# Expert mixture of a hybrid block: accumulator kept turned, 288-token additions, and the further items' round on weights that are still in the ring

## What is computed

```python
# x (1, 512, 1024) float32, 16 meta tokens ahead, D_MODEL 1024, 64 experts, TOP_K 6, D_EXPERT 256
h = layer_norm(concat([meta, x]))
m = hybrid_mixer(h)                      # one projection, HGRN2, RG-LRU, output projection
h = layer_norm(ALPHA * h + m)
scores = sigmoid(h @ router_w)
idx = top_k(scores + router_bias, 6)
wts = scores[idx] / sum(scores[idx]) * 2.5
h = layer_norm(ALPHA * h + swiglu(h, shared) + sum over e in idx of wts_e * swiglu(h, expert e))
# swiglu(x) = (silu(x @ w_gate) * (x @ w_up)) @ w_down
return h[:, 16:]
```

## Time and profile before

| | us |
|---|---|
| median of 3 runs | 1144.53 (1142.01 to 1144.99) |
| the profiled execution: its own time | 1144.19 |
| its span, first to last instruction | 1142.2 |
| first gate and up of an expert pair starts | 589.57 |
| finish starts | 1120.87 |
| PE busy | 1109.3 (97% of the span) |
| DVE busy | 723.1 (63%) |
| moved by DMA | 286.70 MB |

### The profile page before, as it was taken

How to read it: one execution, slowest core, us unless ns; L and a number is a source line. 1 busy time by engine, 2 the same in 40 slices (tenths; PEclk the granted TensorE clock), 3 DMA queues, 4 the chain that set the end, 5 groups by cost and what they waited for, 6 DMA issues and landing times.

```text
span 1142.2 us, 19416 instructions
## 1 busy us (share of the span) xinstructions
PE 1109.3 (97%) x7184; PEld 690.4 (60%) x7184; DVE 723.1 (63%) x1298; ACT 445.4 (39%) x696; POOL 210.3 (18%) x117
## 2 busy tenths in 40 slices
PE   5999999999999999999989999999999999999996
PEld 4889888888888888656534444444444444444443
DVE  7868585858585868685634555555555555555556
ACT  6766665766666656402002112221121122212214
POOL 1443333424243424400010000000000000000000
PEclk9999999999999999999999999999999999999998
DMA  6121212122121303149389999999999999999971
GB/s 241 43 111 42 112 44 110 55 101 78 75 95 60 119 35 134 51 174 376 142 343 419 419 420 421 420 420 419 420 420 420 417 416 416 409 419 415 410 319 78
DMA packets 48323, 286.70 MB, mean 251 GB/s; under 512 B 8994, under 2 KB 10530, under 8 KB 16528
## 3 DMA queue, kind: packets, MB, share of 16 engines
q1 hardware_dynamic: 43088, 272.96, 58.8%
q0 software_dynamic: 5184, 12.98, 2.9%
HBM read 287.62 MB, written 4.19 MB: 255 GB/s over the span
## 4 chain that ended last, share of the span: by engine, by line
PE 52%; DVE 2%; ACT 1%; DMA 1%; issue 0%; POOLq 0%; DVEq 0%
PE pair L1441 22%; PE pair L1504 11%; PE pair L1494 9%; PE pair L935 3%; PE pair L1104 2%; PE pair L186 1%; PE pair L188 1%; DMA xg<-h_rows,idx 1%; PE pair L1452 1%; DVE acc L1648 0%; ACT first L1570 0%; PE pair L1097 0%; DVE table L1326 0%; PE pair L898 0%; PE pair L1118 0%
## 5 line engine op out<-in xcount | busy, mean ns | idle before, releaser
L395 PE MATMUL pair<-hT,w_parts 128*128 128x264 f32 (+1 forms) x2112 | 378.5, 338 | 0.9 <-DVE hT L666 0.5
L395 PEld LDWEIGHTS pair<-hT,w_parts 128*128 128x128 f32 x2112 | 319.7, 189 | 46.5 <-issue 3.8
L242 POOL TENSOR_TENSOR w_parts<-w_raw,w_parts 128x1024 fp32r<-128x1024 f32 x66 | 163.5, 2479 | 295.5 <-ACT w_parts L236 282.1
L1593 DVE TENSOR_TENSOR acc<-acc,pair 128x512 f32<-128x512 f32 x272 | 165.6, 681 | 38.6 <-PE pair L1494 38.6
L1441 PE MATMUL pair<-raw,xgT 128*64 128x512 f32 x768 | 170.3, 595 | 0.1
L927 POOL DMA_INDIRECT xg<-h_rows,idx x36 | 35.9, 997 | 529.9 <-DVE idx L921 461.3
L1441 PEld LDWEIGHTS pair<-raw,xgT 128*64 128x64 f32 x768 | 53.2, 137 | 116.2 <-issue 116.2
L1553 ACT ACTIVATE y_hi<-pair,small 128x512 fp32r<-128x512 f32 x70 | 48.2, 688 | 192.0 <-PE pair L1504 192.0
L1584 DVE TENSOR_TENSOR act_a<-act_s,pair 128x256 f32<-128x256 f32 x35 | 14.8, 422 | 167.9 <-ACT act_s L1546 167.9
L1546 ACT ACTIVATE act_s<-pair 128x256 f32<-128x256 f32 x35 | 13.4, 384 | 224.7 <-PE pair L1441 224.7
L1504 PE MATMUL pair<-raw,aT 128*32 128x512 f32 x768 | 87.4, 595 | 0.0
(11 more groups left out here) (302 smaller groups left out, 1335.0 us busy)
## 6 DMA issues: line engine op xcount, KB each, us to landing
raw<-in_w_gate_up SPq DMA_DIRECT2D x96, 1024.0 KB
raw<-in_w_down SPq DMA_DIRECT2D x48, 1024.0 KB
first<-in_w_gate_up SPq DMA_DIRECT2D x44, 1024.0 KB
w_raw<-in_w_in SPq DMA_DIRECT2D x36, 1024.0 KB, 6.6
first<-in_w_down SPq DMA_DIRECT2D x22, 1024.0 KB
xin<-in_x SPq DMA_DIRECT2D x4, 512.0 KB, 5.5
ws_gu<-in_ws_gate_up SPq DMA_DIRECT2D x1, 2048.0 KB, 7.6
h_rows<-acc SPq DMA_DIRECT2D x4, 512.0 KB, 20.2
```

What stands on the lines that cost most here:

```text
L242: pool.tensor_tensor(w[:, n % PARTS, 1], w_raw[:, n // 2, n % 2], w[:, n % PARTS, 0].bitcast(F32), ALU.subtract).then_inc(sem("w_lo_ready" ...
L395: last = pe.matmul(o, w[:, n % PARTS, pw, k * P:(k + 1) * P], hT[ph][:, k, of], start=(k == 0 and m == 0), stop=(k == KB - 1 and m == 2))
L1593: v.tensor_tensor(part, part, SUM[g], ALU.add).then_inc(sem("sum_free"), 1)
```

## The change

1. **The accumulator is turned.** `accT` holds 8 blocks of 128 columns x 512 tokens (block k has the columns k, k + 8, ...). `scatter` now has y as the stationary side and ST as the moving one: for each block, y_hi and y_lo of the lower halves over tokens 0 to 287 and of the upper halves over tokens 224 to 511. The lower side of one block runs beside the upper side of the next (`first_half`), then they change sides (`second_half`), each two with a wait for `half_done`. The tokens that can go into either half are now 224 to 287. The banks are 4, 5, 1, 7, 6, 2, 3, 0.
2. **Order in a pair.** The look-up stands before `scatter` on PE and before the additions on DVE. Down waits until two additions are done (three were awaited before, ahead of the look-up).
3. **Order of the experts.** The six last places among the 64 are for experts that have further items (from expert 10 on); an expert that stood there changes places. The further items come in the next six places, so that each lies six behind its expert. The loop of SP and POOL stays at `n_rounds` (10 if at most six further items fit so); PE, ACT and DVE run one round more, in which PE waits for no new weights, since those of the round before are still in the ring.
4. **Shared expert.** Its down projection gives 8 turned blocks in place of 4 tiles, added by 8 DVE steps of 512 columns in place of 4 of 1024. h1T is needed for that; so two loads into `first` wait for `shared_taken`.
5. **Tables.** The matmuls with 0/1 tables (`ones_b`, `before_b`, `chosen`) are bf16. There are 160 places for items instead of 136; the steps on DVE that place them are more and wider. The two token columns are no longer in `table` but stay in `table_now`.
6. **The end** turns `accT` back by 8 matmuls of 128 columns a tile and reads y and PSUM in strides.

```diff
-EXTRA = 2 * P * TOP_K // HALF + (T - 2 * P) * TOP_K // SLOTS
-ITEMS = E + EXTRA
+LOW_END, HIGH_AT = 288, 224
+EXTRA = 2 * HIGH_AT * TOP_K // HALF + (LOW_END - HIGH_AT) * TOP_K // SLOTS
...
+ITEMS = E + ROUND + EXTRA
...
-        self.SUM = tuple(banks[n] for n in (4, 5, 6, 7, 1, 2, 3, 0))
+        self.SUM = tuple(banks[n] for n in (4, 5, 1, 7, 6, 2, 3, 0))
...
         sp.wait_ge(sem("shared_up_done"), 4)
+        bring(2, 1, 2)
+        sp.wait_ge(sem("shared_done"), KB)
+        bring(2, 0, 2)
+        sp.wait_ge(sem("shared_taken"), KB)
         for u in range(PAIR):
             bring(2, u, 0)
-        bring(2, 1, 2)
-        sp.wait_ge(sem("shared_done"), TT)
-        bring(2, 0, 2)
...
+            for j in range(2):
+                last = pe.matmul(banks[DOWN_BANK[k]][:, :], ws_dn[:, j, k::KB], aT[:, j], start=(j == 0), stop=(j == 1))
...
-        for t in range(TT):
-            v.wait_ge(sem("shared_done"), t + 1)
-            v.scalar_tensor_tensor(acc[:, t], acc[:, t], ALPHA, pair[DOWN_BANK[t] // 2][:, :], ALU.mult, ALU.add)\
+        for k in range(KB):
+            v.wait_ge(sem("shared_done"), k + 1)
+            v.scalar_tensor_tensor(accT[:, k], h1T[:, k], ALPHA, banks[DOWN_BANK[k]][:, :], ALU.mult, ALU.add)\
...
+                for k in range(KB):
...
+                    pe.matmul(o[k // 4][:, k % 4 * P:(k % 4 + 1) * P], accT[:, k, rows], ident[:], start=(k % 4 == 0),
+                              stop=False, skip_group_check=True)
...
+            def add_in(g, turn):
+                for part in (y_hi, y_lo):
+                    for i in range(2):
+                        of, cols = SIDES[(turn + i) % 2]
+                        last = pe.matmul(SUM[g + i][:, cols], part[of, g + i::KB], ST[b][of, cols],
+                                         start=(turn == 0 and part is y_hi), stop=(turn == 1 and part is y_lo),
+                                         skip_group_check=True)
+                return last
...
+            def second_half(g):
+
+                pe.wait_ge(sem("half_done"), HALVES * p - HALVES + g // 2 + 1)
+                add_in(g, 1).then_inc(sem("sum_done"), 2)
+
+            first_half(0)
+            first_half(2)
+            second_half(0)
+            first_half(4)
+            second_half(2)
+            first_half(6)
+            second_half(4)
+            second_half(6)
...
+            pairs.look_up(pe, p + 3, b)
             scatter(p, (b + 2) % THIRDS)
 
-            pe.wait_ge(sem("sum_free"), ADDS * p + LOOK_AT + 1)
-            pairs.look_up(pe, p + 3, b)
+            pe.wait_ge(sem("sum_free"), ADDS * p + 2)
...
-        finish(THIRDS * n_rounds + 2, 1)
+
+        for h in range(THIRDS):
+            one(THIRDS * n_rounds + h + 2, (h + 2) % THIRDS, n_rounds - 1 + (h > 0), 16 * n_rounds + 32)
+        finish(THIRDS * n_rounds + THIRDS + 2, 1)
...
+                v.scalar_tensor_tensor(by_k(rows), LAST_AT[t][:, :].rearrange("p (k c) -> p c k", k=KB)[:, of_c],
+                                          neg_mean[:, col], by_k(g2[:, part]), ALU.add, ALU.mult))
```

More of the change, by code:

```diff
@@ L1026, in out_and_route @@
     TOT = banks[1][:, TT * E:(TT + 3) * E]
-    numbers = ((0, (0, 1, 2)), (1, (TT - 1,)), (2, (0,)))
+    numbers = [(n, [(t, slice(0, min(P, end - P * t))) for t in range(TT) if end > P * t])
+               for n, end in enumerate((LOW_END, T, HIGH_AT))]
     ROW = 2 * ITEMS
@@ new lines, in _ @@
+        further_before, heavy_before, further_all, heavy_all = (own[:, n:n + 1] for n in range(4))
+        start, stays, more, late_six, rest, shift, more_steps, at = (few[:, n:n + 1] for n in range(8))
+        st.add(v.tensor_tensor(spot, spot, heavy_before, ALU.subtract))
+        st.add(v.scalar_tensor_tensor(start, heavy_before, float(ROUND), further_before, ALU.min, ALU.subtract))
+        st.add(v.scalar_tensor_tensor(stays, heavy_before, float(ROUND), heavy, ALU.is_lt, ALU.mult))
+        st(v.scalar_tensor_tensor(more, heavy_all, float(ROUND), further_all, ALU.min, ALU.subtract))
@@ new lines, in _ @@
+        st.add(v.tensor_scalar(late_six, spot, 0.0, float(ROUND), ALU.is_ge, ALU.mult))
+        st.add(v.tensor_tensor(rest, further, stays, ALU.subtract))
+        st.add(v.tensor_scalar(shift, stays, -float(HALF), -float(HALF), ALU.mult, ALU.add))
+        st.add(v.tensor_scalar(steps, steps6[:], more, None, ALU.is_gt))
+        st(v.tensor_scalar(d1[:], count[:], start, None, ALU.add))
+        st.add(v.tensor_reduce(more_steps, steps, AX, ALU.add))
+        st.add(v.tensor_scalar(d2[:], d1[:], rest, None, ALU.is_lt))
@@ L1392, in experts @@
     parts = lambda t: (slice(0, D),) if t < TT - 1 else (slice(0, D // 2), slice(D // 2, D))
+    by_k = lambda row: row.rearrange("p (c k) -> p c k", k=KB)
+    done = [mem["raw"][:, t // 2, t % 2 * D:(t % 2 + 1) * D] for t in range(TT)]
     @block.sync
@@ L1421, in _ @@
                 sp.wait_ge(sem("out_ready"), i + 1 + (part.start > 0))
-                sp.dma_start(out[t * P:(t + 1) * P, part], acc[:, t, part]).then_inc(sem("stored"), 16)
+                sp.dma_start(out[t * P:(t + 1) * P, part], done[t][:, part]).then_inc(sem("stored"), 16)
         sp.wait_ge(sem("stored"), 16 * (TT + 1))
@@ L1472, in finish @@
                     for part in (y_hi, y_lo):
-                        last = pe.matmul(o[m], ST[b][:, t * P:(t + 1) * P], part[:, m * 512:(m + 1) * 512], start=False,
-                                         stop=(part is y_lo))
+                        last = pe.matmul(o[m].rearrange("p (k c) -> p k c", k=KB // 2), ST[b][:, rows],
+                                         part[:].rearrange("p (c k) -> p k c", k=KB)[:, m * KB // 2:(m + 1) * KB // 2],
+                                         start=False, stop=(part is y_lo), skip_group_check=True)
                 last.then_inc(sem("tile_done"), 1)
@@ L1615, in _ @@
         weigh(0, 0)
-        look_and_part(0, 0)
+        look(0, 0)
+        part_y(0)
         def one(p, b, item):
@@ L1646, in _ @@
             for part in parts(t):
-                rows = acc[:, TILES[t], part]
-                st(v.scalar_tensor_tensor(rows, LAST_AT[t][:, part], neg_mean[:, col], g2[:, part], ALU.add, ALU.mult))
+                rows, of_c = done[t][:, part], slice(part.start // KB, part.stop // KB)
+                st(v.scalar_tensor_tensor(by_k(rows), LAST_AT[t][:, :].rearrange("p (k c) -> p c k", k=KB)[:, of_c],
+                                          neg_mean[:, col], by_k(g2[:, part]), ALU.add, ALU.mult))
                 if t + 1 < TT:
```

217 lines of the change are left out of this document (118 added, 99 removed).

## The result

| us | before | after |
|---|---|---|
| median (before: 1142.01 to 1145.55; after: 1175.57 to 1178.17; 4 runs each) | 1144.76 | 1176.36 |
| span of the profiled execution | 1142.2 | 1176.3 |
| h1T's first use, by the router | 529.04 | 531.89 |
| first gate and up of a pair | 589.57 | 591.67 |
| finish starts | 1120.87 | 1153.39 |

The change makes the kernel slower: the ratio is 1.0283 (95% interval 1.0261 to 1.0304). Of the 34.1 us in the spans, 2.85 arise before the first line that the change touches, the part to the first gate and up takes 0.74 less (59.78 for 60.52), the pairs take 30.4 more (561.7 for 531.3) and the finish 1.6 more (22.95 for 21.36).

The account below looks back on a forecast made before the run. Loads bound the pairs: pair 31's last weights at 1062.0 + 3.0 = 1065.0, next gate-up 11.28 later, three pairs of 14.65, finish at 1120.2 instead of 1120.94. So 0.7 us off 1144.19: 1143.5 us, range 1135.5 to 1149.5.

Parts of the forecast that it names:

- What bounds the kernel: Expert pairs: loads need 15.8 us a pair, PE 15.23; PE lives on a lead of about 18 us.
- two of the signs that were named: Signs of being wrong: PE never waits, last chunk before 1060, additions block over 3 us, finish over 23 us.
- the upper bound of 16.3: Weight loads: time for one pair's loads on the slowest DMA engines, at most 16.3 us; 15.9 was used.
- the way back of 31.8 us: Weight loads: pair 31's second gate-up chunk lands 2 x 15.9 = 31.8 us before pair 33's 1093.85, at 1062.0.
- Part 1: Last round's weights: 18.9 MB, 45 us of the queue, go; still 35 pairs; pair 31 waits for the last weights.
- Part 2: Turned additions in each pair: slots of 140 ns, block 2.5 us instead of 3.08, pair 14.65 us on PE.
- Part 5: Finish: turning the accumulator back takes 1.9 us, as the 1.98 before; strided reads of y and PSUM cost 0.
- Rival (d): Additions: row halves' weight loads go one after the other, pair 16.05, 5.6 us more, 1149.1; chance 0.07.
- Part 3: Refill before the expert pairs: two loads wait longer, nothing moves for 3.0 us, every later chunk lands 3.0 us later.
- Part 4: Tables before the pairs: bf16 gains and more, wider DVE steps cancel; net 0 for tables_read (-1 to +1).
- rival (c): Finish: strided PSUM reads cost 3.2 us and strided moving operands 1.9, giving 1148.6; chance 0.10.
- The sum: Whole kernel: finish starts at 1120.2 instead of 1120.94, 0.7 us won on 1144.19, giving 1143.5 us.

Follow-up runs that it names:

- the run with adjoining columns: The whole change, but each block has 128 adjoining columns, weights laid out to fit, y, ws_down and PSUM read without steps; 1143.56 us, ratio 0.9978 to the kernel before.
- the second trace of the kernel before: The kernel before, unaltered, run once more for its trace; 1147.26 us.

## Why the prediction was wrong

**What bounds the kernel.** Right for the kernel before, and for the change as soon as its loads are quick: the run with adjoining columns has PE ahead of the loads up to pair 18 and then waiting in mid gate and up. For the changed kernel itself it was wrong: two of the signs that were named came, PE never waits and the block takes over 3 us. The landing of pair 31's chunk, 1065.6 in the run with adjoining columns for 1065.0 forecast, is in part luck. Where PE waits the loads come 16.2 us apart, near the upper bound of 16.3 and not at 15.9, but the last two pairs' chunks only 15.0 (PE goes on at 1035.59 in pair 29 and at 1065.6 in pair 31). In the second trace of the kernel before, pair 31's chunk landed 31.5 us ahead of pair 33's (1065.33 and 1096.79), so the way back of 31.8 us was about right there; but in the changed order pair 31 is itself one of the last two and comes sooner. Against that stood a gap of the refill that was over a microsecond longer than forecast.

**Part 1.** Right that the loads go (267.86 MB moved for 286.70) and that there is no seventh further item.

**Part 2, the failed step.** "so 0.45 ns a column and 140 ns for 288": the price of a slot came from rows with adjoining columns, and y's step of eight has no term in it. Part 5 gives the only reason, xg's 195 ns, and that is a row of transposes, whose pace a step leaves as it is. A slot takes 0.241, not 0.140: 16 x 0.101 = 1.6 us a pair, which gives 16.25 for 14.65; 16.14 was measured. So a pair is 0.91 us longer than before instead of 0.58 shorter, and 34 times 0.91 are the pairs' 30.4 us, but for 0.5. All else in this part held: adjoining columns give slots of 0.13 to 0.14, a block of 2.5 to down and a pair of 14.75, and the additions hold up nothing.

**Rival (d)** had nearly the right pair, 16.05, for another reason (loads of two halves one after the other, which the runs rule out), and yet gave 1149.1. It charged 4 pairs. At 16.05 PE is slower than the 15.8 which the prediction had for the loads, so it never waits and all 34 blocks count: 34 x (16.05 - 15.23) = 28 us, 1172. The regime had changed and the sum had not.

**Part 3** was right in kind, too small in size (4.3 to 4.7 us of idle transfer), and showed in the time only where PE was quick enough. **Part 4** was about right (-0.74 for 0; -0.8 to -1.5 in four later traces with the same front, for a lower bound of -1), but as a net of other terms: the tables alone gained 3.2 where they were put at -1 to +1. **Part 5** took 0, and rival (c) had the two strides: the moving operand costs 1.6 us (1.9 there), the PSUM step nothing (3.2 there). **The sum** is 1143.5; with the single term of the step removed from the kernel, in the run with adjoining columns, the time is 1143.56. That it meets the sum so closely is luck, as the kernel before stood at 1146.09 that time: the ratio is 0.9978 where 0.9991 was forecast.

## What to carry to other kernels

Before a layout is chosen, look at which operand is read with a step: in these runs fp32 elements in steps of four or eight about halved the pace of plain stationary loads, steps of eight that of moving operands, and a step of two was free. It costs where the load is what PE goes by; behind a matmul of 0.43 us it costs nothing. When a row serves as evidence that something costs nothing, take one of the very operation that is to be priced, and read its pace and not only its length: xg's transposes kept their pace, and plain loads did not. And when a rival changes which engine is the slow one, count its price over all rounds, not over the few that the main case counts.

## What was not expected of the hardware

- A load of 128 fp32 columns: 184 to 193 ns adjoining or in steps of two; 316 to 336 in steps of four or eight, and then 0.23 to 0.25 us apart, for 64 and for 128 rows. In a transpose 140 and 195, and 0.109 and 0.111 us apart.
- Two loads in different row halves run side by side: two loads and two matmuls of 288 columns in 0.13 us.
- The granted clock falls in the blocks of stepped loads that have fewer matmul columns in the same time: to 0.50 in the last 5 us of the block with two in the same rows (0.67 over all of it). In the changed kernel's own blocks it stays at 1.00. The loads' pace, 0.48 us for two, is the same at 1.00 and at 0.50.
